# Routed experts of a two-layer block: gathered experts first, then all-token experts in row form with the small pairs between them

## The chip, the cores and the metric

The kernel runs on one core of one Trainium2 chip. The metric is the time of one execution on the device in microseconds (us).

## What is computed

Two blocks of two layers each run one after the other on 256 tokens of width 1024. The change touches only the experts of the second block, which both of its layers have:

```
N_EXPERTS = 16; TOP_K = 2; D_EXPERT = 512
def grouped_moe(x, router_w, router_bias, w_gate, w_up, w_down):
    xt = x.reshape(-1, d)
    ...
    combine = jnp.sum(one_hot(expert_idx, 16) * weights[..., None], axis=1)
    y = jnp.zeros(xt.shape)
    for e in range(N_EXPERTS):
        he = silu(xt @ w_gate[e]) * (xt @ w_up[e])
        y = y + combine[:, e:e + 1] * (he @ w_down[e])
    return y
```

Each token picks two experts of 16; `xt` is 256 x 1024, gate and up weights are 1024 x 512, down weights 512 x 1024. The result goes with the residual into a layer norm, and that into the next layer or out. All is float32. A product that needs more than one pass of TensorE's rounded type is made of three: a matrix is split into a high part (a rounded copy) and a low part (what is left), and high x high, high x low and low x high are added up.

## The kernel before

**Tiling.** Tokens lie in two tiles of 128. PSUM is eight banks of 128 x 512 (`PS`); banks 0 to 3 collect the experts' sum for the whole layer, banks 4 to 7 hold what is in work. Weights come from HBM in chunks of 128 x 1024 (512 KB) into `raw`, six places. ACT writes the chunk's high part (`whi`, `w3h`, `w4h`: five places), DVE subtracts and writes the low part (`wlo`, `w3l`, `w4l`).

**Experts by rank.** The router sorts the 16 experts by how many tokens they have. The first three (`ND`) can have any number and see all 256 tokens. The next five (`NL`) have at most 128, 104, 88, 76 and 64 places (`CAPS`); their tokens are gathered by matmuls with a 0/1 matrix (`pick`) into `xgh` and `xgl`, and their outputs scattered back by its transpose (`pickT`). The last eight have at most 64 tokens each and go in four pairs (`NP`): two experts side by side on the halves of the array, in plain float32, so that their weights are not split. A pair chunk is two DMAs of 512 KB into one slot of a ring (`ring`, three slots, `NSLOT`) and eight recorded matmul passes.

**The order.** Each engine runs the order in which its part is written, with semaphores between the engines; nothing is reordered by a scheduler. `gather` makes 32 units, four for each eighth of the width: two for the gathered experts, two for the pairs. Before it twelve small matmuls spread the all-token experts' routing weights over rows (`wrow`). `experts` then has two parts. First twelve steps of the all-token experts, each one 128-wide piece of the hidden width: weights stationary, the 256 tokens moving (`gate_up_half`, L2104), then the down projection (`down`, L2124). Four pair chunks lie between them in each step, in runs of one and two. After three steps a pair is done. Then come the gathered experts, five of them, in a software pipeline (`up_or_gate`, `down_e`, `turn_e`, `scatter`): for expert i up (4 chunks), scatter of i-2, gate (4), down of i-1 (4), then the transposes of i's hidden rows.

**ACT and DVE in the gathered part.** For each expert both engines have fixed duties between the splits of chunks: the silu of the gate (`silu_e`, L880) and the scaling by up and routing weight on DVE (`gated_e`, L1930), both after the last gate chunk; the copy and the subtraction of the transposed hidden rows (`hidden_e`, L884 and L1936); the copy and subtraction of the output (`out_e`). `split_e` (L867, L1923) splits the next chunk in the order of use. How many `split_e` stand ahead of each duty is written in the loop from L921 on. The DMA queue (SP) loads a chunk as soon as the split six chunks earlier is done (`large_load`).

Of the kernel before, what the change touches and what calls it, by code (L numbers as in the profile page):

```python
# [62 lines left out]
TURNS_E = 2  # L63
# [13 lines left out]
STEPS_D = 2 * TURNS_E * ND  # L77
PAIR_CHUNKS = 12
PC = PAIR_CHUNKS * NP
NSLOT = 3  # L80
UNIT_BANKS = (0, 1, 2, 3, 5, 6)
TURN_BANKS = (0, 1, 2, 3, 5)
NC = 12 * NL
PICKED = (NL, NL + 2, NB)
NRAW, NW = 6, 5
# [70 lines left out]
def both_blocks(nc, A, out):  # L156
    ctx = ExitStack()
    with ctx:
# [3 lines left out]
        def sem(name):  # L162
# [17 lines left out]
        wlo = sb("wlo", [P, 3, 1024], F32R)  # L180
        gs = sb("gs", [P, 2, S])
        h32 = sb("h32", [P, 2, S])
        hTh = sb("hTh", [P, 2, S], F32R)
# [22 lines left out]
        at = nc.alloc_sbuf_tensor_at  # L206
        memh = at("memh", [P, KB, S], F32R, offset=proj_at)
# [9 lines left out]
        wrow = at("wrow", [P, ND, S], F32, offset=pairs_at[0] + 4 * KB * 2 * P)  # L217
        ring = [at(f"ring{n}", [P, 1024], F32, offset=o) for n, o in enumerate((
            pairs_at[1] + 4 * KB * 2 * P, RA_at + 4 * (2048 + NB * S), tl_at, tl_at + 4 * 1024, xn_at, xn_at + 4 * 1024))]
        poh = at("poh", [P, 1024], F32R, offset=gain_at)  # L220
        pol = at("pol", [P, 1024], F32R, offset=gain_at + 4 * 1024)
        uw = sb("uw", [P, S])
# [4 lines left out]
        outh = xTh[:].rearrange("p k s -> p (k s)")[:, 0:D]  # L227
        outl = xTl[:].rearrange("p k s -> p (k s)")[:, 0:D]
        out2h = xTh[:].rearrange("p k s -> p (k s)")[:, D:2 * D]
        out2l = xTl[:].rearrange("p k s -> p (k s)")[:, D:2 * D]  # L230
        out_of = lambda i: (out2h, out2l, UB) if i == NL - 1 else (outh, outl, 6)
# [137 lines left out]
        ln_in = sem("ln_in")  # L369
# [96 lines left out]
        wrow_ready = sem("wrow_ready")  # L466
# [11 lines left out]
        def down_end(i):  # L478

            return 12 * i + 20 if i < NL - 1 else NC  # L480

# [6 lines left out]

        def e_w(n):

            if n % NW < 3:
                return whi[:, n % NW], wlo[:, n % NW]
            return (w3h[:], w3l[:]) if n % NW == 3 else (w4h[:], w4l[:])
# [22 lines left out]
        def _(sp):  # L516
# [44 lines left out]
            with sp.Fori(0, DEPTH) as l:  # L561
# [27 lines left out]
                sp.dma_start(par[:, 0], A["ln_x_w"][l].partition_broadcast(P)).then_inc(ln_in, 16)  # L589
                sp.dma_start(par[:, 1], A["ln_x_b"][l].partition_broadcast(P)).then_inc(ln_in, 16)  # L590
# [30 lines left out]
            for l in range(DEPTH):  # L621
# [37 lines left out]
                t0 = 4 * TURNS_FFN + ND * TURNS_E * l  # L659
                t_end = t0 + ND * TURNS_E  # L660
# [10 lines left out]

                at_d = [None]
                at_p = [None, None]

                def dense_load(u, m):

                    if u % (2 * TURNS_E) == 0 and m == 0:
                        at_d[0] = chosen(u // (2 * TURNS_E))
                    cols = slice(u % (2 * TURNS_E) * P, (u % (2 * TURNS_E) + 1) * P)
                    if m < 2:  # L680
                        src = w[("e_gate", "e_up")[m]][at_d[0]].rearrange("o (k p) f -> p (o k) f", p=P)[:, :, cols]
                    else:
                        src = w["e_down"][at_d[0], cols, :].rearrange("o f n -> f (o n)")
                    step_load(m, t0 + u // 2, u % 2, src)

                def pair_load(c):

                    p, part, slot = c // PAIR_CHUNKS, c % PAIR_CHUNKS, c % NSLOT
# [3 lines left out]
                    if c >= NSLOT:  # L692
                        hold(sp, p_used, PC * l + c - NSLOT + 1)
                    elif c:
                        hold(sp, gat_psum, UNITS * (l + 1))
                    for e in range(2):
                        dst = ring[2 * slot + e][:]
# [4 lines left out]

                n = 0
                at_l = [None, None]

                def large_load():

                    nonlocal n
# [2173 lines left out]
```

## Time and profile before

| | |
|---|---|
| time, median of 3 runs | 2420.82 us (2416.68 to 2422.79) |
| profiled execution: time, span | 2423.87 us, 2421.7 us |
| TensorE matmul busy | 2294.5 us, 95% |
| VectorE (DVE), ScalarE (ACT) busy | 1418.9 us (59%), 982.4 us (41%) |
| HBM read | 451.56 MB, 187 GB/s over the span |
| TensorE's granted clock, mean | 0.985 of full |
| one layer's expert stage | 311 us, twice |

The page is read from its first part, which gives the engines' shares, to the timeline, which gives for one engine the instructions in order of time with the idle time before them and who ended it. In the timeline a float32 matmul stands as two records, so "x8" is one pair chunk of four matmuls. A record's length reaches past the start of the next one, since matmuls are pipelined: what a matmul costs is the distance of starts. "PEclk" is the clock that TensorE was granted, where 1.00 is 2.4 GHz and 0.50 is 1.2 GHz.

### The profile page before, as it was taken

The page shows a single profiled execution, that of the slowest core. Times are in us where ns is not written, and L with a number is a line of the kernel's source. Part 1 is how long each engine was busy: PE and PEld are TensorE (multiplying, and loading weights), DVE is VectorE, ACT ScalarE, POOL GpSimd, SP SyncE. Part 2 cuts the span into 40 slices and gives each one's busy share as a digit, 9 for nine tenths or more (in the row PEclk, how much of TensorE's full clock was granted, in tenths as well). Part 3 has the DMA queues.
Part 4 walks back from the last instruction along what each step waited for, and adds up shares of the span by engine and source line. Part 5 has one row for each costly group of instructions (what it writes and reads, how often), then busy time and mean ns, then how long its engine had stood idle before and what let it go on. Part 6 is the DMA issues. An engine that isn't in the chain of part 4 may idle for free.

```text
span 2421.7 us, 37290 instructions
## 1 busy us (share of the span) xinstructions
PE 2294.5 (95%) x13918; PEld 1878.9 (78%) x13918; DVE 1418.9 (59%) x1893; ACT 982.4 (41%) x1245; POOL 101.6 (4%) x82
## 2 busy tenths in 40 slices
PE   9999999999999999999999898999999889999997
PEld 7998888899899888889988576866666677666664
DVE  5666767666666567666664356633348565533377
ACT  5554522444555453244443234332237333322264
POOL 0000023000000003200000000000000000000000
PEclk9999999999999999999999999999999999999998
DMA  6667501566566761046656242489989441599985
GB/s 194 187 187 218 169 10 35 170 186 182 158 182 185 222 192 44 1 145 186 187 178 189 91 157 91 148 287 338 331 297 335 163 157 61 193 340 342 316 307 205
DMA packets 386961, 458.02 MB, mean 189 GB/s; under 512 B 18542, under 2 KB 273170, under 8 KB 386706
## 3 DMA queue, kind: packets, MB, share of 16 engines
q1 hardware_dynamic: 381824, 446.35, 57.5%
q10 hardware_dynamic: 5010, 9.98, 1.3%
q8 instruction: 79, 1.29, 0.2%
q14 instruction: 48, 0.39, 0.0%
HBM read 451.56 MB, written 1.05 MB: 187 GB/s over the span
## 4 chain that ended last, share of the span: by engine, by line
PE 49%; issue 37%; DVE 7%; DMA 2%; POOL 2%; ACT 2%; SPq 1%; ACTq 0%; DVEq 0%; POOLq 0%; PEldq 0%
PE PS L2306 4%; PE PS L2114 4%; PE PS L2116 3%; PE PS L2115 3%; PE PS L2310 2%; PE PS L2392 2%; PE PS L2133 2%; PE PS L2394 2%; PE PS L2393 2%; PE PS L2134 2%; PE PS L2135 2%; PE PS L2243 2%; PE PS L2245 1%; PE PS L2244 1%; PE PS L2686 1%
## 5 line engine op out<-in xcount | busy, mean ns | idle before, releaser
L1312 DVE TENSOR_TENSOR wlo<-raw,whi 128x1024 fp32r<-128x1024 f32 x336 | 410.2, 1224 | 446.6 <-ACT whi L828 443.6
L828 ACT ACTIVATE whi<-raw 128x1024 fp32r<-128x1024 f32 x336 | 354.2, 1057 | 501.0 <-PE PS L2116 379.0
L2114 PE MATMUL PS<-xTh,whi 128*128 128x256 f32 x1792 | 512.8, 286 | 5.6 <-DVE xTl L1279 4.0
L2115 PE MATMUL PS<-xTl,whi 128*128 128x256 f32 x1792 | 506.8, 283 | 0.0
L2116 PE MATMUL PS<-xTh,wlo 128*128 128x256 f32 x1792 | 506.7, 283 | 0.0
L2114 PEld LDWEIGHTS PS<-xTh,whi 128*128 128x128 f32 x1792 | 343.0, 191 | 41.8 <-issue 32.7
L2115 PEld LDWEIGHTS PS<-xTl,whi 128*128 128x128 f32 x1792 | 343.2, 192 | 3.2
L2116 PEld LDWEIGHTS PS<-xTh,wlo 128*128 128x128 f32 x1792 | 343.2, 191 | 0.0
L2392 PE MATMUL PS<-whi,xTh 128*128 128x416 f32 (+2 forms) x480 | 181.9, 379 | 18.5 <-DVE xTl L1279 7.5
L2133 PE MATMUL PS<-whi,hTh 128*128 128x512 f32 x448 | 179.0, 400 | 4.3 <-DVE wlo L1312 4.3
L2394 PE MATMUL PS<-whi,xTl 128*128 128x416 f32 (+2 forms) x480 | 177.3, 369 | 0.0
L2393 PE MATMUL PS<-wlo,xTh 128*128 128x416 f32 (+2 forms) x480 | 176.5, 368 | 0.0
L2134 PE MATMUL PS<-wlo,hTh 128*128 128x512 f32 x448 | 175.9, 393 | 0.0
L2135 PE MATMUL PS<-whi,hTl 128*128 128x512 f32 x448 | 174.4, 389 | 0.0
L1305 DVE TENSOR_TENSOR wlo<-raw,whi 128x1024 fp32r<-128x1024 f32 (+2 forms) x92 | 107.3, 1177 | 108.7 <-ACT whi L841 107.3
L841 ACT ACTIVATE whi<-raw 128x1024 fp32r<-128x1024 f32 (+2 forms) x92 | 91.2, 1019 | 149.9 <-PE PS L2394 101.2
L2306 PE MATMUL PS<-ring,xgp 128*64 128x512 f32 x512 | 120.7, 602 | 4.1 <-DMA ring<-in_l_e_up_dram 3.6
L2392 PEld LDWEIGHTS PS<-whi,xTh 128*128 128x128 f32 x480 | 91.2, 190 | 38.6 <-issue 9.9
L2133 PEld LDWEIGHTS PS<-whi,hTh 128*128 128x128 f32 x448 | 84.4, 188 | 39.4 <-issue 17.8
L1376 DVE TENSOR_TENSOR wlo<-raw,whi 128x832 fp32r<-128x832 f32 (+1 forms) x80 | 83.6, 1063 | 53.5 <-ACT whi L979 50.9
L979 ACT ACTIVATE whi<-raw 128x832 fp32r<-128x832 f32 (+1 forms) x80 | 73.5, 930 | 100.9 <-PE PS L2394 51.6
L852 ACT ACTIVATE gs<-RB 128x256 f32<-128x256 f32 x88 | 37.0, 420 | 157.2 <-DVE RB L1321 157.2
(516 smaller groups left out, 3875.2 us busy)
## 6 DMA issues: line engine op xcount, KB each, us to landing
raw<-in_ffn_w_gate_dram SPq DMA_DIRECT2D x88, 512.0 KB, 5.3
raw<-in_ffn_w_up_dram SPq DMA_DIRECT2D x88, 512.0 KB, 6.3
raw<-in_ffn_w_down_dram SPq DMA_DIRECT2D x88, 512.0 KB, 3.7
raw<-in_l_e_gate_dram SPq DMA_DIRECT2D x64, 512.0 KB, 6.0
raw<-in_l_e_up_dram SPq DMA_DIRECT2D x64, 512.0 KB, 6.4
raw<-in_l_e_down_dram SPq DMA_DIRECT2D x64, 512.0 KB, 5.6
ring<-in_l_e_up_dram SPq DMA_DIRECT2D x64, 512.0 KB, 6.5
ring<-in_l_e_gate_dram SPq DMA_DIRECT2D x64, 512.0 KB, 6.7
```

The lines of the kernel that those rows point to most:

```text
L828: nc.scalar.activation(whi[:, m if slot is None else slot], raw[:, m, j], ACT.Copy).then_inc(hi_done[m], 1)
L1312: nc.vector.tensor_tensor(wlo[:, w], raw[:, m, j], whi[:, w].bitcast(F32), ALU.subtract).then_inc(lo_done[m], 1)
L2114: mm(out_, whi[:, m, ks], xTh[:, k, :], start=(k == 0), stop=False)
L2115: mm(out_, whi[:, m, ks], xTl[:, k, :], start=False, stop=False)
L2116: last = mm(out_, wlo[:, m, ks], xTh[:, k, :], start=False, stop=(k == KB - 1))
L2133: mm(out_, hTh[:, j, ts], whi[:, slot, ns], start=opens, stop=False, skip_group_check=True)
L2134: mm(out_, hTh[:, j, ts], wlo[:, slot, ns], start=False, stop=False, skip_group_check=True)
L2135: last = mm(out_, hTl[:, j, ts], whi[:, slot, ns], start=False, stop=False, skip_group_check=True)
L2306: last = mm(PS[rows, 6 + c // 4, :], xgp[p // 2][:, kk_, c0:c0 + HALF], ring[2 * slot + e][:, cs], start=(kk_ == 0), stop=(kk_ == KB - 1), ...
L2392: mm(out_, of[0][:, k, ts], whi[:, at[c], ws], start=(k == 0), stop=False)
L2393: mm(out_, of[0][:, k, ts], wlo[:, at[c], ws], start=False, stop=False)
L2394: last = mm(out_, of[1][:, k, ts], whi[:, at[c], ws], start=False, stop=(k == KB - 1))
```

## The change

The experts' two parts change places, and the all-token experts take another form.

- **Gather.** The twelve spreading matmuls and the copies into `wrow` are gone. The 16 units of the gathered experts come first, then the 16 of the pairs. The first split of weights no longer stands before the copies of `pickT`; three splits lie between the units' copies (after units 14, 20, 26 on ACT, 15, 21, 27 on DVE).
- **One chunk order.** `part_of` numbers 96 chunks of `raw`: 60 of the gathered experts and 36 of the all-token experts (12 each: 4 gate, 4 up, 4 down), dense chunk 0 between the last two down projections. Up to chunk 55 the five places for split chunks are used, then three (`w_slot`), since the other two become ring slots.
- **Row form.** `dense_part` holds the tokens stationary and moves 512 columns of weights: gate into banks 4 and 5, silu to `hd`, then up into the same banks; both are multiplied with the routing weight as a per-row scalar (`gated_d`), eight transposes (`dense_turn`), then down.
- **Pairs.** Five ring slots instead of three. The table `CPS` says how many of the 48 pair chunks follow each of the dense chunks 1 to 35, before and after a `dense_turn`; there are 22 runs, of which ten have three chunks. Slots 1 to 4 open as the tiles that they lie on fall free at the end of the gathered part.

```diff
-NSLOT = 3
+NSLOT = 5
+CPS = ((0, 0), (3, 0), (0, 0), (3, 0), (2, 0), (0, 0), (2, 0), (1, 1), (0, 0), (3, 0), (0, 0), (3, 0),
...
-NC = 12 * NL
+NC = PARTS * (NL + ND)
+N_DENSE = PARTS * NL - 4
...
+        def w_slot(n):
+            return n % 5 if n < N_DENSE else (n - N_DENSE + 1) % 3
```

ACT in the expert stage; DVE's code has the same sequence:

```diff
-                pair_out(NP - 1)
-                for i in range(NL + 1):
-                    if i < NL:
-                        if i:
-                            split_e()
-                            split_e()
-                            if i == 1:
-                                silu_e(0)
-                            hidden_e(i - 1)
...
-                        for _ in range(4 if i else 6):
-                            split_e()
-                        if i:
-                            split_e()
-                            split_e()
-                            silu_e(i)
-                            split_e()
-                            split_e()
...
+                for u in range(0, UNITS, 2):
+                    act.wait_ge(gat_psum, UNITS * l + u + 1)
+                    dst = xgh[:, u // 2] if u < 2 * KB else xgp[0][:, u // 2 - KB]
+                    nc.scalar.activation(dst, PS[:, UNIT_BANKS[u % 6], 0:dst.shape[1]], ACT.Copy).then_inc(gat_hi, 1)
+                    if u in (14, 20, 26):
                         split_e()
+                split_e(3)
+                for i in range(1, NL):
+                    split_e(2)
+                    if i == 1:
+                        silu_e(0)
+                    hidden_e(i - 1)
+                    split_e(2)
+                    if i > 1:
                         out_e(i - 2)
+                    split_e(6)
+                    silu_e(i)
+                    split_e(2)
+                split_e(4)
+                hidden_e(NL - 1)
+                out_e(NL - 2)
+                split_e(5)
+                out_e(NL - 1)
+                split_e()
```

TensorE's all-token chunk and its order:

```diff
+                    if part < 8:
+                        for k in range(2):
+                            kk_, ws = 2 * (part % 4) + k, slice(k * 512, (k + 1) * 512)
+                            for t in range(NT):
+                                ts = slice(t * P, (t + 1) * P)
+                                mm(PS[:, 4 + t, :], xTh[:, kk_, ts], hi[:, ws], start=(kk_ == 0), stop=False)
+                                mm(PS[:, 4 + t, :], xTh[:, kk_, ts], lo[:, ws], start=False, stop=False)
+                                last = mm(PS[:, 4 + t, :], xTl[:, kk_, ts], hi[:, ws], start=False, stop=(kk_ == KB - 1))
...
-                for p in range(NP):
-                    for s in range(3):
-                        u = 3 * p + s
-                        gate_up_half(t0 + u // 2, u % 2, 0)
...
+                for i in range(NL):
+                    up_or_gate(i, UB)
...
+                    up_or_gate(i, GB)
                     assert n == gate_end(i)
                     if i:
                         down_e(i - 1)
+                    turn_e(i)
+                dense_part(0)
+                scatter(NL - 2)
+                down_e(NL - 1)
+                for q in range(1, NQ):
+                    dense_part(q)
+                    if q == 1:
+                        scatter(NL - 1)
+                    if q in TURN_Q:
+                        pair_turn(TURN_Q.index(q))
+                    if q in SCATTER_Q:
+                        pair_scatter(SCATTER_Q.index(q))
+                    c = FIRST_CP[q]
+                    for k in range(CPS[q][0]):
+                        pair_chunk(c + k)
+                    if q % PARTS == 7:
+                        dense_turn(q // PARTS)
+                    for k in range(CPS[q][1]):
+                        pair_chunk(c + CPS[q][0] + k)
```

Two places of the order show what stands in a row. ACT before, around the silu (`gs`, 104 rows) and the copy of the transposed hidden rows (`hTh`) of gathered expert 1; chunk n goes to `whi` for n mod 5 of 0, 1, 2, to `w3h` for 3, to `w4h` for 4:

```order
L877 ACTIVATE w3h<-raw 128x1024
L877 ACTIVATE w4h<-raw 128x1024
L877 ACTIVATE whi<-raw 128x1024 x3
L882 ACTIVATE gs<-PS 104x512
L877 ACTIVATE w3h<-raw 128x1024
L877 ACTIVATE w4h<-raw 128x1024
L877 ACTIVATE whi<-raw 128x1024 x2
L886 ACTIVATE hTh<-PS 128x416
L877 ACTIVATE whi<-raw 128x1024
L877 ACTIVATE w3h<-raw 128x1024
L891 ACTIVATE xTh<-PS 128x1024
```

Ahead of the silu chunk 17 is split, and chunks 18 to 21 lie between silu and copy. The same place of ACT after the change:

```order
L892 ACTIVATE whi<-raw 128x1024 x3
L892 ACTIVATE w3h<-raw 128x1024
L892 ACTIVATE w4h<-raw 128x1024
L892 ACTIVATE whi<-raw 128x1024
L897 ACTIVATE gs<-PS 104x512
L892 ACTIVATE whi<-raw 128x1024 x2
L892 ACTIVATE w3h<-raw 128x1024
L892 ACTIVATE w4h<-raw 128x1024
L901 ACTIVATE hTh<-PS 128x416
L892 ACTIVATE whi<-raw 128x1024 x2
L905 ACTIVATE outh<-PS 128x1024
```

Ahead of the silu chunk 15 is split, the last of expert 1's gate, and chunks 16 to 19 lie between silu and copy. TensorE before, a single pair chunk (ring tiles against `xgp`) between the two kinds of all-token matmul:

```order
L2115 MATMUL PS<-xTl,whi 128x256
L2116 MATMUL PS<-xTh,wlo 128x256
L2306 MATMUL PS<-ring_66,xgp_60 64x512
L2306 MATMUL PS<-ring_67,xgp_60 64x512
L2306 MATMUL PS<-ring_66,xgp_60 64x512
L2306 MATMUL PS<-ring_67,xgp_60 64x512
L2133 MATMUL PS<-whi,hTh 128x512
L2134 MATMUL PS<-wlo,hTh 128x512
```

One chunk is four matmuls, and the down step follows. TensorE after the change, the first run of three chunks, behind dense chunk 1 and the scatter of the last gathered expert:

```order
L2340 MATMUL PS<-ring_0_63,xgp_61 64x512
L2340 MATMUL PS<-ring_1_64,xgp_61 64x512
L2340 MATMUL PS<-ring_0_63,xgp_61 64x512
L2340 MATMUL PS<-ring_1_64,xgp_61 64x512
L2340 MATMUL PS<-ring_0_65,xgp_61 64x512
L2340 MATMUL PS<-ring_1_66,xgp_61 64x512
L2340 MATMUL PS<-ring_0_65,xgp_61 64x512
L2340 MATMUL PS<-ring_1_66,xgp_61 64x512
L2340 MATMUL PS<-ring_0_67,xgp_61 64x512
L2340 MATMUL PS<-ring_1_68,xgp_61 64x512
L2340 MATMUL PS<-ring_0_67,xgp_61 64x512
L2340 MATMUL PS<-ring_1_68,xgp_61 64x512
```

Three slots of the ring are used up in one run, then dense chunk 2 follows.

## Rows read from the trace of the kernel before

**Rows 1.** Timeline of PE, both expert stretches (start us, us, ..., [idle before]).
```profile
1585.44 0.35 PE L2114 MATMUL PS<-xTh,whi 128*128 128x256 f32 x1 [0.67 <-ACT xgp L1245]
...
1896.15 0.39 PE L2288 MATMUL PS<-xTl,pickT 64*128 64x512 f32 x1
...
2097.64 0.35 PE L2114 MATMUL PS<-xTh,whi 128*128 128x256 f32 x1 [0.67 <-ACT xgp L1245]
...
2408.23 0.39 PE L2288 MATMUL PS<-xTl,pickT 64*128 64x512 f32 x1
```

**Rows 2.** Timeline of PE, a pair chunk, a down step, two pair chunks.
```profile
1762.99 1.94 PE L2306 MATMUL PS<-ring,xgp 128*64 128x512 f32 x8
1764.85 0.50 PE L2133 MATMUL PS<-whi,hTh 128*128 128x512 f32 x1
...
1767.80 3.65 PE L2306 MATMUL PS<-ring,xgp 128*64 128x512 f32 x16
```

**Rows 3.** Timeline of PE, matmuls of a gathered expert, twelve starts apart.
```profile
1802.31 0.40 PE L2243 MATMUL PS<-whi,xgh 128*128 128x512 f32 x1
...
1805.11 0.40 PE L2243 MATMUL PS<-whi,xgh 128*128 128x512 f32 x1
```

**Rows 4.** Timeline of PE, two waits for DVE in layer 0.
```profile
1796.19 0.50 PE L2243 MATMUL PS<-whi,xgh 128*128 128x512 f32 x1 [2.47 <-DVE wlo L1927]
...
1886.29 0.45 PE L2265 MATMUL PS<-whi,hTh 128*64 128x512 f32 x1 [1.51 <-DVE hTl L1939]
```

**Rows 5.** Timelines of PE, ACT, DVE behind the first gathered expert's transposes.
```profile
1808.13 0.66 PE L2277 MATMUL PS<-tab,h 128*128 128x128 f32 x4 [1.47 <-DVE h L1933]
1808.54 0.48 PE L2243 MATMUL PS<-w3h,xgh 128*104 128x512 f32 x1
...
1811.68 0.48 PE L2243 MATMUL PS<-whi,xgh 128*104 128x512 f32 x1
...
1808.82 0.60 ACT L886 ACTIVATE hTh<-PS 128x512 fp32r<-128x512 f32 x1 [1.53 <-PE PS L2277]
...
1810.40 2.36 DVE L1927 TENSOR_TENSOR wlo<-raw,whi 128x1024 fp32r<-128x1024 f32 x2 [0.26 <-ACT whi L877]
```

**Rows 6.** Timelines of PE and ACT behind the second gathered expert's gate.
```profile
1820.10 0.40 PE L2265 MATMUL PS<-whi,hTh 128*128 128x512 f32 x1
...
1823.16 0.50 PE L2265 MATMUL PS<-w3h,hTh 128*128 128x512 f32 x1
...
1820.30 0.60 ACT L882 ACTIVATE gs<-PS 104x512 f32<-104x512 f32 x1 [1.26 <-PE PS L2245]
```

**Rows 7.** Timeline of PE, head of the gather in layer 0.
```profile
1562.99 1.50 PE L2189 MATMUL PS<-tab,par 128*128 128x128 f32 x12
...
1568.73 0.73 PE L2217 MATMUL PS<-pick,xrh 128*128 128x460 f32 x2 [1.57 <-ACT pickT L1238]
```

**Rows 8.** Groups of instructions by line and shape (xcount | busy us, mean ns).
```profile
L1970 DVE SCALAR_TENSOR_TENSOR par<-par,PS 128x512 f32<-128x512 f32 x4 | 3.0, 749 | 7.4 <-ACT par L906 7.4
```

**Rows 9.** Busy time by window (us, engines, PEclk, DMA share, GB/s).
```profile
1600.00:1620.00 20.00, 20.00 (x120) 13.01 (x117) 5.95 (x8) 4.04 (x5) 0.00 (x0) 1.00 1.06 369
```

**Rows 10.** Timeline of PE, two waits elsewhere in the kernel.
```profile
834.77 0.46 PE L2392 MATMUL PS<-whi,xTh 128*128 128x416 f32 x1 [3.19 <-DVE xTl L1279]
...
1308.14 1.10 PE L2686 MATMUL PS<-tl,raw 128*128 128x256 f32 x4 [2.78 <-DMA raw<-in_l_xkv_dram]
```

**Rows 11.** Busy time by window, behind those two waits.
```profile
835.00:836.00 1.00, 1.00 (x5) 0.96 (x5) 1.00 (x4) 1.00 (x4) 0.00 (x0) 0.65 0.99 349
836.00:837.00 1.00, 1.00 (x5) 0.95 (x4) 1.00 (x4) 0.58 (x1) 0.00 (x0) 0.50 0.86 305
837.00:838.00 1.00, 1.00 (x5) 0.95 (x4) 1.00 (x2) 0.00 (x0) 0.00 (x0) 0.50 0.20 75
838.00:839.00 1.00, 1.00 (x5) 0.96 (x4) 0.00 (x0) 0.10 (x1) 0.00 (x0) 0.64 0.00 0
1309.00:1310.00 1.00, 1.00 (x7) 0.87 (x6) 0.71 (x4) 0.16 (x1) 0.00 (x0) 1.00 1.06 412
```

More of the change, by code:

```diff
@@ L751, in _ @@
-                while n < NC:
-                    large_load()
+                while n < NRAW:
+                    part_load()
+                pair_load(0)
+                while n < N_DENSE + 4:
+                    part_load()
+                pair_load(1)
+                pair_load(2)
+                part_load()
+                part_load()
+                pair_load(3)
+                pair_load(4)
+                while n < N_DENSE + 12:
+                    part_load()
+                for step in range(1, NQ):
+                    if n < NC:
+                        part_load()
+                    for c in range(FIRST_CP[step], FIRST_CP[step] + sum(CPS[step])):
+                        if c + NSLOT < PC:
+                            pair_load(c + NSLOT)
@@ new lines, in experts @@
+                split_e(4)
+                hidden_e(NL - 1)
+                out_e(NL - 2)
+                split_e(5)
+                out_e(NL - 1)
+                split_e()
+                for q in range(1, NQ):
+                    if q % PARTS == 7:
+                        gated_d(q // PARTS)
+                    if n < NC:
+                        split_e()
+                    c = FIRST_CP[q]
+                    for k in range(CPS[q][0]):
+                        pair_step(c + k)
+                    if q % PARTS == 7:
+                        hidden_d(q // PARTS)
+                    for k in range(CPS[q][1]):
+                        pair_step(c + CPS[q][0] + k)
@@ L2205, in gather @@
                 for u in range(UNITS):
[L2206 to L2208 removed]
+                    k, bank = u // 2 % KB, UNIT_BANKS[u % 6]
+                    ks = slice(k * P, (k + 1) * P)
                     if u < 6:
@@ L2305, in pair_chunk @@
                                 kk_, c0 = 2 * (c % 4) + k, P * (p % 2) + HALF * e
-                                last = mm(PS[rows, 6 + c // 4, :], xgp[p // 2][:, kk_, c0:c0 + HALF], ring[2 * slot + e][:, cs], start=(kk_ == 0), stop=(kk_ == KB - 1),
+                                last = mm(PS[rows, 6 + c // 4, :], xgp[p // 2][:, kk_, c0:c0 + HALF], ring[slot][e][:, cs], start=(kk_ == 0), stop=(kk_ == KB - 1),
                                           skip_group_check=True)
@@ L2349, in experts @@
[L2349 to L2354 removed]
+                for i in range(NL):
+                    up_or_gate(i, UB)
+                    if i == 0:
+                        pe.wait_ge(gat_hi, UNITS // 2 * (l + 1))
+                        pe.wait_ge(gat_lo, UNITS // 2 * (l + 1))
+                    else:
```

541 lines of the change are left out of this document (238 added, 303 removed).

## Prediction, made before the changed kernel was run

> **What bounds the kernel now.** I read the page first: TensorE is busy for 95% of the span, DVE for 59%, ACT for 41%. Then the timeline of TensorE over the expert stage of each of the two layers, since the change touches that alone. Each stretch lasts 310.9 us from its first matmul to its last (1585.44 to 1896.15, 2097.64 to 2408.23, and 0.2 to the end of the issue slot) [rows 1]. Inside, TensorE goes from matmul to matmul with few holes. DMA moves up to 369 GB/s in a window where TensorE never waits [rows 9], so the transfers keep up but have little to spare. So the bound is TensorE's own order, and the question for the change is twofold: how much TensorE work the new order has, and where TensorE now waits for the split of a weight chunk (ACT writes the high part, DVE subtracts to get the low part).
>
> **Prices on TensorE.** Twelve matmuls of 512 columns start over 2.80 us (1802.31 to 1805.11), 0.233 each, in longer stretches 0.2325; a large chunk of six takes 1.39, a dense chunk of twelve 2.79 [rows 3]. A pair chunk takes 1.86 from its start to the next group's (1762.99 to 1764.85); the record of two chunks is 3.65 against 1.94, so a further chunk adds 1.71. The down step behind it takes 2.95 instead of 2.79 [rows 2]. So each run of pair chunks costs 0.15 + 0.15 beside 1.71 a chunk.
>
> **The gathered experts, in the new place but first without new waits.** Expert 0: 48 matmuls, 11.2, then its transposes with the wait of 1.47 and 0.41 to the next start [rows 5]: 13.1. From 1808.54 [rows 5] the three rounds and the fourth, up to the start of the down projection of expert 4 at 1886.29 [rows 4], take 77.7 in the layer before, and stay. Then dense chunk 0 (2.8), a scatter of eight (1.9) and the last down projection (5.6). Sum 101.1.
>
> **The mixed stage.** 35 dense chunks at 2.79: 97.7. 48 pair chunks at 1.71: 82.1. By the table CPS they lie in 22 runs, 22 x 0.30 = 6.6 (before: 32 runs). Four scatters of pairs and one of a gathered expert, 8 x 0.2325 each: 9.3. Four groups of four transposes at 0.4 [rows 5] and three of eight at 0.8: 4.0. Sum 199.7. Added wait: the all-token hidden rows now need two scalings of 0.75 [rows 8] before their transposes; for experts 0 and 1 a pair chunk of 1.86 covers them, for expert 2 only four transposes do, so 1.5 + 0.2 - 0.4 = 1.3. The copies behind the transposes (two of ACT at 0.60 [rows 5], two of DVE) lie beside one or two pair chunks and add nothing; without that cover they would add some 1.5 each. Together 201.0.
>
> So without new waits a layer's experts would take 302.1, 8.8 less than 310.9. What goes are stalls of the layer before, such as 2.47 before the third large chunk [rows 4], and ten switches between the kinds; the wait of 1.51 before the last down projection [rows 4] stays and is in the 77.7.
>
> **The lead that is lost.** This is the step that decides. ACT and DVE work strictly in the order written. Before, ACT has split 18 large chunks when it comes to the silu of expert 1, and 22 when it comes to the copy of that round's transposes; TensorE has then used 16 and 20. It runs on over two chunks (2.8) while ACT and DVE do silu, scaling and the next split. The order view of the changed kernel shows ACT with 16 and 20 at these places: the first loop now does 6 splits before expert 1 instead of 8 and nothing restores the two. The first chunk that TensorE wants stands behind the silu (or the copy) on ACT, and behind the scaling (or the subtraction) on DVE. The rows of before hold the price, since there the third chunk takes that very way. Behind the transposes of expert 0 the wanted start is 1808.54; ACT's copy starts at 1808.82, DVE's first split behind it runs from 1810.40, and the third chunk starts at 1811.68: 3.14 later [rows 5]. Behind the gate of expert 1 the wanted start is 1820.10, silu starts at 1820.30, the third chunk at 1823.16: 3.06 later [rows 6]. After the change the first chunk starts there. Four gates (experts 1 to 4) and four transposes (0 to 3; narrower copies, so a little less, 3.0) give 8 x 3.04 = 24.3 a layer. Two smaller things cancel: the third chunk no longer waits its 3.04 - 2.79 = 0.25 eight times (-2.0), but where ACT and DVE also move an expert's output (three times) DVE has three pieces of 1.13 apart before the third chunk against 2.79 of TensorE (+1.8). Nothing else has to wait on TensorE's behalf in that time: DMA gains from it.
>
> A layer's experts: 302.1 + 24.3 - 0.2 = 326.2, against 310.9: +15.3, twice +30.6.
>
> **The gather.** Removed: the twelve small matmuls that spread the routing weights (1.50 busy, 1.34 from start to start), the wait of 1.57 for ACT's copies, which stood behind two weight splits [rows 7], and 0.67 before the first matmul, which waited for the last gathered tile [rows 1]; it now writes another bank. Layer 0: -3.6. In layer 1 TensorE did not wait for ACT's copies: -2.0. Now ACT and DVE make three splits inside the gather; six banks lie between a unit and its reuse, so I take nothing. At the end the first token tile is signalled six matmuls before the end instead of four: -0.5 a layer. Together -6.6.
>
> **DMA.** The mixed stage takes 50.3 MB of pairs and 18.3 MB of dense weights in 201 us, 341 GB/s, of which five pair chunks and three dense ones (6.8 MB) can be there at its start. The ring of five pair slots gives every load at least 12.8 us from the release of its slot to its use by the prices above; three pair chunks at 369 GB/s [rows 9] take 8.5. The layer before had the lead of three slots. I take no wait; the bound is that each of the ten runs of three waits half a microsecond, 5 a layer.
>
> **TensorE's clock.** Sixteen new waits of about 2.9 as the profile counts them (start to start 3.3 less the record of 0.39). Elsewhere a wait of 3.19 is followed by a granted clock of 0.65, 0.50, 0.50, 0.64, which is 1.2 GHz for about 3.4 us and costs 1.7; a wait of 2.78 is followed by 1.00, 2.4 GHz [rows 10, 11]. The new waits lie between, nearer the lower. I take two or three falls in sixteen: +4. Ends: none (0), all sixteen (+27). The Trainium skill (TensorE: Matmul & The Clock Gate, HAM oscillation) describes a matmul stream that falls to the half clock at every tile since a wait stands between its bursts. By that page the term would be near +27, by the rows it is near 0 to +4.
>
> **Sum.** +30.6 - 6.6 + 4 = +28. The profiled execution has a span of 2421.7 and a time of 2423.87, 3 above the median of 2420.82; so 2449.7 for the span and 2449 for the median.
>
> **Rivals.**
> The clock falls often. If eight or more of the sixteen waits end in the slow level, it costs 14 to 27 instead of 4: 2459 to 2472. For it speaks that 2.9 is close to 3.19; against it that 2.78 left the clock alone. The page of the Trainium skill named above would give its upper end; the trace lies between the two.
> DMA cannot feed the runs of three. Ten waits of 0.5 a layer: +10, 2459. For it: 341 wanted against 369 at best. Against it: five slots where the layer before ran with three, and no load that is asked for later than 12.8 before its use.
> The lead does not bind (the other side). If TensorE still finds the first chunk split, neither the 48.6 of both layers' waits nor the 4 of the clock are paid, and the time is 2420.8 - 17.6 - 6.6 = 2397. It decides by one thing: whether ACT stands two chunks ahead at a silu. The order view says it does not. If only one of the two places bound (the gates, say), 24.3 and half the clock's 4 would go, about 2423: no change.
>
> **Chances.** Forecast as described (2440 to 2456) 0.72; clock falls often 0.10; DMA or another unseen wait 0.11; one place only 0.03; lead does not bind 0.04. The range that holds 8 in 10 takes in the clock's and DMA's lower cases: 2438 to 2462. A measurement here tells 0.3%, 7 us, from no change. Slower 0.93, same 0.03, faster 0.04.
>
> **What the changed profile would show.** Right: four rows of TensorE per layer with about 2.9 idle before a down projection (releaser DVE's split) and four before an up projection; experts' stretch near 326; no such waits later. TensorE's busy share falls from 95% to about 93%. The granted clock in the gathered stage tells rival one; idle before pair chunks with a DMA as releaser tells rival two. Wrong: large chunks that start at once behind a gate.

## The result, and the profile after

The changed kernel is slower: 1.0242 of the time before, 95% interval 1.0208 to 1.0276. Its median over four executions is 2479.12 us against 2418.75 for the kernel before; one of the four, 3293.09, was disturbed: the ratio leaves it out, and the median of the other three is 2474.56. The profiled execution took 2483.68, its span is 2481.9; before, the span was 2421.7. So 60.2 us are to be found in the two traces. The forecast was +28.

First the page of the changed kernel: its span, the busy time of the engines, and the rows of PE, PEclk and GB/s over 40 equal slices.

```profile
span 2481.9 us, 36018 instructions
...
PE 2315.3 (93%) x13338; PEld 1868.3 (75%) x13366; DVE 1396.7 (56%) x1821; ACT 984.1 (40%) x1241; POOL 101.6 (4%) x82
...
PE   9999999999999999999999899888999898888997
...
PEclk9999999999999999999999899988999999988999
...
GB/s 190 190 188 226 146 1 59 173 191 185 156 183 190 221 153 7 43 186 178 187 173 160 98 136 115 212 228 266 380 339 253 144 128 99 195 227 307 365 345 158
```

TensorE is busy for 93% of the span instead of 95%, as forecast. The new dips lie in the slices in which the gathered experts stand (from 1577 and from 2124; a slice is 62 us). Transfers now come in a hill: up to 380 GB/s averaged over a slice, in the mixed stage; before, they ran at 322 and 315 GB/s over the whole of the experts' stretches.

Next the busy time by window, one window for each stage of the changed kernel (window, its length, PE busy with the number of matmuls, granted clock, DMA share, GB/s): the kernel up to the gather, the gather, the gathered experts of layer 0, the mixed stage of layer 0, what lies between the layers, then gathered experts and mixed stage of layer 1, and the end.

```profile
0.00:1557.45 1557.45, 1485.15 (x9566) 0.99 0.51 149
1557.45:1576.56 19.11, 19.11 (x167) 1.00 0.75 257
1576.56:1705.11 128.55, 102.96 (x382) 0.85 0.67 228
...
1715.37:1924.07 208.70, 204.26 (x885) 0.98 0.86 315
1924.07:2123.59 199.52, 178.01 (x990) 0.98 0.36 120
2123.59:2249.28 125.69, 100.10 (x383) 0.88 0.68 229
...
2259.53:2469.27 209.74, 205.25 (x885) 0.98 0.83 306
2469.27:2481.90 12.63, 0.00 (x0) 0.63 0.21 83
```

With the 10.3 of dense chunk 0, the scatter and the last down projection (left out between the stages), the experts take 347.5 and 345.7, against 310.7 and 310.6 before [rows 1]: 71.9 of loss, of which the rest of the kernel gives 11.7 back. Three things stand in the two rows of the gathered experts. PE is busy for 103 of 128.55 us; the granted clock is 0.85 and 0.88; and the time of the two layers differs by 2.9 though they do the same work, which goes with the difference of their clocks. The same stretch before ran at 1.00.

The waits of TensorE in the gathered experts of layer 0 (waited for, total us, times, longest), and behind "..." those of the rest of the layer's experts:

```profile
PE PS L2254 <- DVE wlo L1930: 8.9, 3, 3.0
PE PS L2235 <- DVE wlo L1930: 5.6, 2, 2.8
PE PS L2254 <- DVE w3l L1930: 3.0, 1, 3.0
PE PS L2235 <- DVE w3l L1930: 2.9, 1, 2.9
PE PS L2235 <- DVE w4l L1930: 2.7, 1, 2.7
PE PS L2266 <- DVE h L1936: 1.5, 1, 1.5
...
PE PS L2276 <- DVE outl L1947: 3.3, 1, 3.3
PE PS L2323 <- DVE hd L1953: 1.1, 1, 1.1
```

The first five rows are the eight waits of the forecast: four before a down projection (L2254), four before an up projection (L2235), 2.72 to 2.98 each, for the low part of a split chunk. Layer 1 has the same eight. They answer to the single waits of [rows 4]. The row of L2276 was not forecast: the scatter of the last gathered expert waits 3.3 us.

What a wait leaves behind it, in the timeline of PE: the first rows after the wait of 2.89, and after the one before that scatter.

```profile
1592.91 0.75 PE L2235 MATMUL PS<-w3h,xgh 128*104 128x512 f32 x1 [2.89 <-DVE w3l L1930]
1593.46 0.63 PE L2236 MATMUL PS<-w3l,xgh 128*104 128x512 f32 x1
1593.88 0.63 PE L2237 MATMUL PS<-w3h,xgl 128*104 128x512 f32 x1
...
1599.17 0.39 PE L2235 MATMUL PS<-whi,xgh 128*104 128x512 f32 x1
...
1721.57 0.67 PE L2276 MATMUL PS<-outh,pickT 64*128 64x512 f32 x1 [3.31 <-DVE outl L1947]
```

From start to start a matmul takes 0.42 to 0.43 instead of 0.23, until 1598.6: TensorE runs at 1.2 GHz instead of 2.4, with a granted clock of 0.50 from 1592.0 to 1598.8.

### The profile page after: what moved, and what is told of

The parts are those of the page before. It is cut to its first block, busy times and chain, and to the rows that moved or that the text cites. A ratio compares the mean times of both kernels' runs of the same rounds, so it can differ in the third digit from the quotient of the medians.

```text
span 2481.9 us, 36018 instructions
## 1 busy us (share of the span) xinstructions
PE 2315.3 (93%) x13338; PEld 1868.3 (75%) x13366; DVE 1396.7 (56%) x1821; ACT 984.1 (40%) x1241; POOL 101.6 (4%) x82
## 4 chain that ended last, share of the span: by engine, by line
PE 51%; issue 37%; DVE 7%; ACT 2%; POOL 2%; DMA 1%; SPq 1%; ACTq 0%; DVEq 0%; POOLq 0%; PEldq 0%
PE PS L2340 5%; PE PS L2344 2%; PE PS L2297 2%; PE PS L2416 2%; PE PS L2235 2%; PE PS L2418 2%; PE PS L2237 2%; PE PS L2417 2%; PE PS L2236 2%; PE PS L2298 2%; PE PS L2119 2%; PE PS L2118 2%; PE PS L2117 2%; PE PS L2299 2%; PE PS L2710 1%
## 5 line engine op out<-in xcount | busy, mean ns | idle before, releaser
L1322 DVE TENSOR_TENSOR wlo<-raw,whi 128x1024 fp32r<-128x1024 f32 x264 | 322.2, 1223 | 225.5 <-ACT whi L846 222.4
L2117 PE MATMUL PS<-xTh,whi 128*128 128x256 f32 x1408 | 399.9, 284 | 4.5 <-DVE xTl L1289 4.3
L2119 PE MATMUL PS<-xTh,wlo 128*128 128x256 f32 x1408 | 399.1, 283 | 0.0
L2118 PE MATMUL PS<-xTl,whi 128*128 128x256 f32 x1408 | 399.1, 283 | 0.0
L846 ACT ACTIVATE whi<-raw 128x1024 fp32r<-128x1024 f32 x264 | 277.4, 1053 | 227.1 <-PE PS L2119 218.8
L1930 DVE TENSOR_TENSOR wlo<-raw,whi 128x1024 fp32r<-128x1024 f32 x148 | 177.9, 1221 | 252.9 <-ACT whi L892 252.9
L2117 PEld LDWEIGHTS PS<-xTh,whi 128*128 128x128 f32 x1408 | 270.6, 192 | 9.0 <-DVE xTl L1289 5.3
L2118 PEld LDWEIGHTS PS<-xTl,whi 128*128 128x128 f32 x1408 | 270.6, 192 | 3.2
L2119 PEld LDWEIGHTS PS<-xTh,wlo 128*128 128x128 f32 x1408 | 270.6, 192 | 0.0
L892 ACT ACTIVATE whi<-raw 128x1024 fp32r<-128x1024 f32 x148 | 153.4, 1054 | 261.1 <-PE PS L2299 169.8
L2136 PE MATMUL PS<-whi,hTh 128*128 128x512 f32 x352 | 139.0, 395 | 4.4 <-DVE wlo L1322 4.4
L2137 PE MATMUL PS<-wlo,hTh 128*128 128x512 f32 x352 | 138.0, 392 | 0.0
```

The lines of the kernel that those rows point to most:

```text
L846: nc.scalar.activation(whi[:, m if slot is None else slot], raw[:, m, j], ACT.Copy).then_inc(hi_done[m], 1)
L892: nc.scalar.activation(e_w(n)[0], e_raw(n), ACT.Copy).then_inc(e_hi, 1)
L1322: nc.vector.tensor_tensor(wlo[:, w], raw[:, m, j], whi[:, w].bitcast(F32), ALU.subtract).then_inc(lo_done[m], 1)
L1930: TTop(e_w(n)[1], e_raw(n), e_w(n)[0].bitcast(F32), ALU.subtract).then_inc(e_lo, 1)
L2117: mm(out_, whi[:, m, ks], xTh[:, k, :], start=(k == 0), stop=False)
L2118: mm(out_, whi[:, m, ks], xTl[:, k, :], start=False, stop=False)
```

## The experiments

The theory: the lost lead of two split chunks makes the eight waits a layer, and the waits bring the clock down. The rivals: the new order or its transfers cost the time and the waits are a symptom; or the clock falls for a reason of its own. A third question is the unforeseen scatter wait. ACT's and DVE's programs have the same order of splits, so each edit of it is shown once and stands in both.

### The lead given back

```diff
-split_e(3)
+split_e(5)
 for i in range(1, NL):
     ...
-split_e(4)
+split_e(2)
 hidden_e(NL - 1)
```

> The changed kernel with its two split chunks given back: on ACT and on VectorE five large chunks are split between the gather and the loop over the gathered experts instead of three, and two instead of four behind that loop. TensorE's program is untouched. Theory (lost lead, and a clock that falls behind the waits): the sixteen waits of about 3.0 us from start to start go (48.6), and with them the stretches at the lower clock that stand behind fifteen of them in the trace (13 to 16 us a layer in the profiled execution); the third chunk of a group waits 0.25 again (+4). From 2477 that gives 2400 to 2412, granted clock back at 0.983 or more. Rival (the waits alone; the clock falls for another reason of the new order): 2428 to 2433 with the clock still near 0.972. Rival (transfers): the lead only moves the wait to the landing of the raw chunks, above 2440, with DMA named before ACT's splits. The wait of 3.3 before the scatter of the last gathered expert stays in all of them.

Measured: 2407.65, ratio 0.9947 (0.9924 to 0.9971) to the kernel before, granted clock 0.984. The gathered experts take 90.46 and 90.47 instead of 128.55 and 125.69; between the transposes of expert 0 and those of expert 4 no wait longer than 0.2 us is left. The theory's range holds it; both rivals are out. The same TensorE program is some 70 us faster with two chunks of lead, and faster than the kernel before.

### The scatter of the last gathered expert, alone

```diff
-split_e(5)
+split_e(4)
 out_e(NL - 1)
-split_e()
+split_e(2)
```

> The changed kernel with one thing moved: behind the loop over the gathered experts ACT and VectorE split four chunks, then move the output of the last gathered expert, then split two, instead of five, the output, one. It is the price of the one wait that the forecast did not name: TensorE stands 3.31 and 3.36 us before the scatter of that output (releaser VectorE's outl), and the next 8 scatter matmuls and the pair chunks behind them run at 0.64 to 0.67 of the clock. Theory (the output stands behind a split whose raw chunk lands late, since four pair loads are ahead of it): the wait and its clock go, 3.3 + 3.3 to 4.3 a layer, so 2477 - 14 = 2463 (2460 to 2466). Rival (the output is late by itself, two moves of 1.1 to 1.3 and the semaphores between them): the wait only shrinks, and 2474 to 2478 stays.

Measured: 2468.39 (2464.76 to 2472.81), a little above what was expected, ratio 1.0208 (1.0180 to 1.0236). The intervals of this ratio and of the changed kernel's overlap, so the times alone do not settle it. The trace does: the mixed stage is 202.14 and 202.15 instead of 208.70 and 209.74, at clock 1.00 instead of 0.98. The windows of the mixed stage of both layers:

```profile
1708.93:1911.07 202.14, 201.01 (x886) 1.00 0.88 325
...
2248.20:2450.35 202.15, 201.01 (x885) 1.00 0.85 315
```

So the place costs 6.6 and 7.6, 14.2 in all, about half of it the wait.

### Both edits

> Both edits together: two split chunks of lead for the gathered experts, and the output of the last gathered expert one split earlier. TensorE's program is that of the changed kernel. If the two places are independent and hold all that the change lost, the time is that of the sum without new waits, 2 x 302.1 for the experts (before: 2 x 310.9) and some 7 to 12 less in the gather and at the ends: 2388 to 2396, about 1% under the kernel before. Rival (the new order costs more than its count of matmuls, through transfers or the runs of three pair chunks): above 2405, with idle time of TensorE before pair chunks or dense chunks in the mixed stage.

Measured: 2392.57, ratio 0.9893 (0.9864 to 0.9923). Busy time by window of this kernel, gathered experts and mixed stage of both layers:

```profile
1573.06:1663.57 90.51, 87.34 (x383) 1.00 0.91 321
...
1673.80:1875.94 202.14, 201.01 (x886) 1.00 0.88 327
...
2075.27:2165.77 90.50, 87.31 (x383) 1.00 0.91 321
...
2176.00:2378.15 202.15, 201.02 (x885) 1.00 0.86 317
```

A layer's experts take 302.9, which is the cost of the new order by itself. The forecast's count was 302.1. The rival (the new order costs more than its matmuls) is out: TensorE is busy for 201.0 of 202.1 us of the mixed stage.

### The waits filled

```diff
 pe.wait_ge(eo_lo, NB * l + i)
+if i < NL - 1:
+    warm(11, 6)
...
 turn_e(i)
+if i < NL - 1:
+    warm(11, UB)
...
 if q == 1:
+    for _ in range(11):
+        mm(PS[:, 0, :], zero[:, 0:P], zero[:], start=False, stop=False, skip_group_check=True)
     scatter(NL - 1)
```

Here `warm(n, bank)` issues n matmuls on zeros into a bank that is free at that place.

> The changed kernel with its waits as they are, but TensorE has work in them: eleven matmuls on zeros (bf16, 512 columns, about 0.24 us each, 2.6 us together) before the down projections of gathered experts 0 to 3, before the up projections of experts 1 to 4, and before the scatter of the last one; they add nothing to the result. They fit into the waits of 2.7 to 3.3, so the real matmuls start at the same moment as before. It separates the two parts of a wait: the standing itself, and the stretch at the lower clock behind it. Theory (half of what the change lost is the clock, 27 to 36 us in all): 2441 to 2452, granted clock back at 0.983 or more while ACT and VectorE keep their times. Rival (the lower clock behind the waits costs little, since the splits would have held TensorE anyway): 2470 to 2477 with a clock near 0.985. Rival (the clock falls whatever stands in the waits): 2477, clock 0.972.

Measured: 2452.90, ratio 1.0149 (1.0119 to 1.0180), granted clock 0.990. First the timeline of PE at the first filled wait, then the windows of the gathered experts of both layers.

```profile
1580.43 2.54 PE L2080 MATMUL PS<-zero 128*128 128x512 bf16 x11
1583.49 0.48 PE L2235 MATMUL PS<-w3h,xgh 128*104 128x512 f32 x1 [0.52 <-DVE w3l L1930]
1583.81 0.39 PE L2236 MATMUL PS<-w3l,xgh 128*104 128x512 f32 x1
...
1567.14:1681.64 114.50, 107.14 (x471) 1.00 0.71 247
...
2100.39:2214.84 114.45, 107.12 (x470) 1.00 0.72 247
```

The real matmul still starts 3.06 after the first zero one, and the next one is at full speed. The gathered experts take 114.5 in both layers. So the whole parts into three: 90.5 of work, 24.0 of waiting (114.5 - 90.5), and 14.0 and 11.2 of lower clock (128.55 - 114.50, 125.69 - 114.45). The clock's theory holds, though the median is 1 above its range. The fill did nothing for the scatter: there the zeros took 2.55 of a wait that grew to 5.0 (a wait of 2.48 is left behind them), and the mixed stage still took 208.8. TensorE had come sooner and the scatter could not: what it waits for comes at a time of its own.

### Why the scatter waits

```diff
 pair_load(1)
 pair_load(2)
 part_load()
 part_load()
+part_load()
+part_load()
 pair_load(3)
 pair_load(4)
```

> The kernel with its lead given back, and one more edit on the loading queue alone: two raw chunks (the second and third of the first dense expert's gate) are asked for before the fourth and fifth pair chunks instead of behind them. ACT's and VectorE's programs stay, so the output of the last gathered expert still stands behind the split of the third dense chunk. Theory (that split waits 4.16 for its raw chunk, which landed 10 us after it was asked for, behind the pair loads, so the wait before the scatter is a transfer's): the wait of 3.7 and the clock behind it go, 7.0 a layer in the trace, 2407.7 - 14 = 2394. Rival (the order on ACT and VectorE is the cause, whenever the chunk lands): 2407. Rival (DMA moves 388 GB/s there and is full, so that the delay only moves to a pair chunk): 2400 to 2407 with idle time before a pair chunk.

Measured: 2391.79, ratio 0.9891 (0.9874 to 0.9907); the mixed stage is 202.1. ACT's timeline, in the kernel with the lead alone (first two rows) and in this one (last two): a split, and the high part of the last output behind it.

```profile
1679.29 1.06 ACT L892 ACTIVATE whi<-raw 128x1024 fp32r<-128x1024 f32 x1 [4.51 <-DMA raw<-in_l_e_gate_dram]
1680.25 1.00 ACT L905 ACTIVATE outh<-PS 64x1024 fp32r<-64x1024 f32 x1
```

```profile
1671.43 1.06 ACT L894 ACTIVATE whi<-raw 128x1024 fp32r<-128x1024 f32 x1 [0.32 <-PE PS L2258]
1672.75 1.02 ACT L907 ACTIVATE outh<-PS 64x1024 fp32r<-64x1024 f32 x1 [0.26 <-PE PS L2258]
```

The split in front of the output waited 4.51 for a raw chunk. With that chunk asked for before two of the pair loads, it is there and the output follows at once. So the wait belonged to the loading order: a transfer behind four pair loads, a split that waits for it, an output behind the split, the scatter behind the output. Two links were cut, each alone: the first here, and the third where the output was moved one split earlier. The rival that the full DMA would move the delay to a pair chunk is out: no pair chunk waits.

### The lead taken from the kernel before

```diff
-for _ in range(4 if i else 6):
+for _ in range(4):
     split_e()
 ...
-    for _ in range(3):
+    for _ in range(5):
         split_e()
     hidden_e(i - 1)
```

> The kernel before, with the edit that the change made to the lead and nothing else: four large chunks are split ahead of expert 1 instead of six, two more ahead of the last hidden rows. Order on TensorE, buffers and transfers are those of before. Theory (the lead by itself costs what the change lost in the gathered experts): a layer gets the eight waits (24.0 by the run with filled waits, 114.5 less 90.5) and the clock behind them (11 to 14): 35 to 38 a layer, so 2419 + 73 = 2489 to 2495, with a granted clock near 0.97. Rival (the waits belong to the new place or buffers of the gathered experts, not to the lead): 2419 to 2425.

Measured: 2487.78, ratio 1.0294 (1.0274 to 1.0314), +70. The waits of TensorE in its gathered experts of layer 0:

```profile
PE PS L2265 <- DVE wlo L1927: 8.9, 3, 3.0
PE PS L2243 <- DVE wlo L1927: 5.6, 2, 2.8
PE PS L2265 <- DVE w3l L1927: 3.0, 1, 3.0
PE PS L2243 <- DVE w3l L1927: 2.9, 1, 2.9
PE PS L2243 <- DVE w4l L1927: 2.7, 1, 2.7
```

Row for row these are the waits of the changed kernel. The rival (they belong to the new place or its buffers) is out. The time is 1 us under the range that was expected.

### A lead of one chunk

The two edits, with `split_e(4)` and `split_e(3)` around the loop in place of 5 and 2.

> Lead of one chunk instead of none or two: both earlier edits together, but with four chunks split ahead of the loop and three behind it. The chunk that TensorE wants after a gate or the transposes is then split, the next one is not. Theory (a wait is 3.04 less what TensorE can still do, 1.39 for one chunk): 1.65 before the second chunk instead of 3.04 before the first, eight times a layer, 13.2; and such a short wait, below the 2.78 that left the clock alone in the kernel before, costs no clock. From 2392.6: 2419 (2415 to 2422), clock near 0.988. Rival (any hole in this stream costs the clock its 1.5 again): 2440 to 2446, clock near 0.975. Rival (the splits catch up by themselves, as one chunk is enough): 2393 to 2396.

Measured: 2417.07, ratio 0.9996 (0.9982 to 1.0010). Three rows of TensorE's waits in the gathered experts of layer 0, and the windows of that stretch in both layers:

```profile
PE PS L2235 <- DVE wlo L1930: 3.6, 4, 1.4
PE PS L2254 <- DVE wlo L1930: 3.0, 2, 1.5
PE PS L2235 <- DVE w3l L1930: 1.8, 2, 1.4
...
1570.93:1674.35 103.42, 87.95 (x383) 1.00 0.80 275
2089.35:2192.79 103.44, 88.01 (x382) 1.00 0.80 277
```

The waits are 1.33 to 1.53 and cost 12.9 a layer (103.4 - 90.5; expected 13.2). The clock stays at 1.00 through all sixteen. So in both layers together the first missing chunk costs 26 us of waiting (24.5 in the medians), the second another 22 of waiting and 25 of clock.

### How often, and how long, a wait must be to cost the clock

One wait a layer (the first kernel of this part: both edits, and the lead taken away at the gate of expert 2 only):

```diff
-split_e(6)
+split_e(4 if i == 2 else 6)
 silu_e(i)
-split_e(2)
+split_e(4 if i == 2 else 2)
```

> Both earlier edits together (two chunks of lead, output one split earlier), and then the lead taken away at one place a layer only, the gate of expert 2: two of the six splits ahead of its silu now stand behind it. One wait of about 3.0 a layer in a stretch where TensorE otherwise never stands. It asks if the clock falls behind one such wait, or only where they come every 14 us. Theory (each wait of 2.9 as the profile counts it is enough): a first record above 0.6 us behind it, granted clock 0.5 to 0.75 in the window after it, 4.5 a layer, about 2401. Rival (a single wait leaves the clock alone, as the one of 2.78 did in the kernel before, and the falls of the changed kernel come from their frequency): 1.00 behind it, 3.0 a layer, about 2398.

Measured: 2397.01 in one execution. The timeline of PE at the wait, in layer 0 and in layer 1, two rows each:

```profile
1618.94 0.45 PE L2254 MATMUL PS<-w3h,hTh 128*104 128x512 f32 x1 [2.98 <-DVE w3l L1930]
1619.23 0.39 PE L2255 MATMUL PS<-w3l,hTh 128*104 128x512 f32 x1
...
2123.01 0.73 PE L2254 MATMUL PS<-w3h,hTh 128*104 128x512 f32 x1 [2.98 <-DVE w3l L1930]
2123.54 0.63 PE L2255 MATMUL PS<-w3l,hTh 128*104 128x512 f32 x1
```

The same wait at the same place of the program: once the clock stays, once it falls. Neither theory nor rival is right. The length of a wait does not decide alone. Other single waits in the traces say the same. The first row below is from the changed kernel, early in the program, and the clock stays at 1.00 behind it. The second is from the kernel with four ring slots (below), at the very place of the wait of 2.78 in [rows 10], and the clock behind it is 0.50 until 1316.6:

```profile
211.34 0.46 PE L2416 MATMUL PS<-whi,xTh 128*128 128x416 f32 x1 [3.05 <-DVE xTl L1289]
...
1310.66 0.76 PE L2709 MATMUL PS<-tl,raw 128*128 128x256 f32 x1 [2.92 <-DMA raw<-in_l_xkv_dram]
```

Then shorter waits, sixteen of them again: the changed kernel with the output moved, and `warm(3, ...)` or `warm(1, ...)` in place of eleven, none before the scatter.

> The changed kernel with the output of the last gathered expert one split earlier (2468 by its own run) and its lead still missing, and three matmuls on zeros (0.24 us each, 0.7 together) in each of the sixteen waits instead of eleven. TensorE starts its real work at the same moment; it stands 2.0 to 2.3 instead of 2.7 to 3.0. It asks how long a hole of this stream costs the clock. Known so far: with 0.35 to 0.5 and with 1.4 to 1.5 nothing was lost, with 2.72 to 2.98 the clock was lost 48 times in 50. Theory (a hole must be near three microseconds long): no loss, the 25 to 28 us of the clock come back, 2441 (2438 to 2446). Rival (a hole of two is enough): 2464 to 2470, granted clock near 0.974.

> As the run with three, but one matmul on zeros (0.24 us) in each wait: TensorE stands 2.4 to 2.7. Theory of a sharp length: either all of the falls stay (2465) or all go (2441). Rival (it depends on where the hole lies, as the two layers of the run with one hole showed for one and the same wait of 2.98): some of the sixteen fall, in between.

Measured: 2464.67 (ratio 1.0196, 1.0167 to 1.0224) with three, and 2461.91 in one execution with one. The windows of the gathered experts, with three zeros:

```profile
1576.98:1699.89 122.91, 102.62 (x401) 0.90 0.69 234
2112.30:2235.72 123.42, 103.13 (x401) 0.90 0.70 233
```

The idle times are 2.07 to 2.24 there (2.50 to 2.89 with one zero matmul), and 8.4 and 9.0 above the 114.5 of the filled waits remain, at clock 0.90. The theory (a wait must be near three microseconds) fell; the time lies in the rival's range. In the trace the clock is below full in 13 of 16 such intervals with three zeros, and in 13 of 16 with one. So with one zero, too, neither all falls stayed nor all went; its rival (some of them) holds.

### The slack of the transfers

Both edits, with `NSLOT = 4` and without the fifth early pair load.

> Both earlier edits together (2392.6), with four slots for pair chunks instead of five. It measures the slack of the transfers in the mixed stage, where DMA moves 331 to 391 GB/s and TensorE waits for no pair chunk. By the counts a load then has 3 pair chunks and 2 dense ones (10.9 us) at the tightest between the release of its slot and its use, and three pair chunks at 369 GB/s take 8.5. Theory (the ring has a slot to spare): no change, 2390 to 2396. Rival (DMA is the next bound, and the five slots are what hides it): TensorE waits before pair chunks with DMA as the releaser, 5 us a layer or more, 2402 and above.

Measured: 2396.43 (2386.72 to 2400.61), ratio 0.9896 (0.9861 to 0.9931). The mixed stage of layer 0:

```profile
1681.69:1883.85 202.16, 201.03 (x885) 114.47 (x886) 59.64 (x57) 51.39 (x59) 0.00 (x0) 1.00 0.89 327
```

202.16 with four slots, 202.14 with five. The ring has a slot to spare. The median is 0.4 above the range of the theory and the executions spread by 14 us; the profiled one lost 29.0 us to the lower clock ahead of the gather, against 18.8 in that of the kernel with five slots.

## Why the forecast was wrong, step by step

The direction and the deciding mechanism were right, the size was not: +28 against some +60. In the profiled executions, us for both layers:

| step | forecast | measured | from |
|---|---|---|---|
| work of the new order, without the new waits | -17.6 | -15.5 | 302.9 a layer against 310.65 |
| waits of the lost lead | +48.2 | +47.9 | 114.5 - 90.5 |
| the clock behind them | +4 | +25.3 | 14.05 + 11.24 |
| scatter of the last gathered expert | 0 | +14.2 | 6.6 + 7.6 |
| gather, between the layers, end, and what lies ahead of the gather | -6.6 | -11.7 | windows before and after |
| sum | +28 | +60.2 | |

**What bounds the kernel, and the prices.** Right. TensorE's own order is the bound, and counted matmuls at the prices of [rows 2] and [rows 3] gave 302.1 for a layer that takes 302.9. The mixed stage takes 1.1 more than counted, and the gathered part gives 0.4 back. Runs of three pair chunks take 5.30, of two 3.58, of one 1.87, as 0.15 + 1.71 a chunk says.

**The lost lead.** Right, in place, number and size: eight a layer, 24.1 forecast, 24.0 measured, from the 3.14 and 3.06 of [rows 5] and [rows 6]. The restored lead, the half lead and the old order without its lead each give the cost that this working gives.

**The clock.** This term failed: two or three falls in sixteen were taken, 4 us; it was 25. The bounds (0 to 27) held it, and so did the rival "the clock falls often", which had a chance of 0.10. The step that failed is the reading of [rows 10, 11]: a wait of 3.19 with a fall and one of 2.78 without were read as two sides of a length. They were two single waits, far from others. Behind waits of 2.72 to 2.98 that come two to a round of some 28 us, the clock was below full in 47 of 48 intervals (the changed kernel, the one with the output moved, the old order without lead); behind one such wait a layer in one case of two; behind waits of 2.07 to 2.24 in 13 of 16; behind waits of 1.33 to 1.53 in none of 16. That the wait of 2.78 kept the clock was no sign of its length: 2.92 at the same place in another kernel's trace did not, and 3.05 elsewhere did. The Trainium skill (TensorE: Matmul & The Clock Gate, HAM oscillation) describes a stream of bursts with a wait between them and the clock down at each; its waits, for transfers, are longer (3 to 5 us). The waits of 2.72 to 2.98 here behave like it, at 25 of the 27 that were worked out as its end; those of 1.33 to 1.53 do not. The clock events of the traces add up to 18.8 and 15.4 us of lost clock in the two stretches, but the cost was 14.0 and 11.2. Of the difference, 1.5 and 1.3 lie inside the waits, where TensorE does nothing. Some more is that a slow first chunk gives ACT and DVE the time for the third, before which TensorE stands 0.4 us three times a layer in the kernel with filled waits; the rest stays open.

**The scatter.** The forecast had its eight matmuls and no wait. It looked for the limit of the transfers in the runs of three pair chunks and gave each load there 12.8 us; that was right, and a run with one slot fewer changed nothing. But it did not follow the raw chunks past the new place of the pair loads in the loading queue. One of them lands 13.6 us after it is asked for in layer 0 and 11.3 in layer 1, and its split stands ahead of an output that TensorE wants. The wait is 3.3, and the clock behind it doubles the price. The forecast counted for the lead what stands behind a waiting instruction, and did not do it here.

**The gather and the rest.** Forecast -3.6, -2.0 and -0.5 twice. The gather of layer 0 went from 24.47 to 19.11, -5.4; before, it held one fall of the clock (0.93 granted, 1.7 us), after none, so the removed work is worth 3.7. Between the layers, with the gather of layer 1: 201.49 to 199.52, -2.0. Another 3.5 lie ahead of the gather, where both programs are the same (1560.97 and 1557.45); they are no effect of the change, but 3.4 of lost clock (25.6 and 22.2). The last 0.8 are at the end (13.47 and 12.63).

**The range.** 2438 to 2462 held the forecast's clock and DMA cases one at a time. Each unknown had its bound in the text (27 for the clock, 10 for transfers), but with the clock at 25 and a transfer's wait together the time is above both.

## What to carry to other kernels

When work is moved, count at every point where a strictly ordered engine turns from preparing to something else how many prepared pieces lie ahead, and compare it with before; one number, 18 or 16 splits ahead of a silu, was worth 70 us here, and was not part of what the change was about. Where a wait of TensorE of about three microseconds comes back every ten to twenty, count the lower clock behind each one: here it cost 1.6 us a wait, and still 1.1 where the waits were 2.1 to 2.2. Do not read a threshold from two single waits. A load that is put into a shared queue delays everything behind it, so follow the next raw chunk to its split and to what stands behind the split.

## What the runs showed of the hardware

- In the gathered experts, waits of 1.33 to 1.53 us left the granted clock at 1.00 sixteen times out of sixteen; waits of 2.07 to 2.24 did not in thirteen of sixteen. Nothing between was tried there. The same wait of 2.98 at the same instruction of two layers ended once at full and once at half clock.
- These are no thresholds for other places. The wait of 2.47 in [rows 4], once a layer in the kernel before, left the clock at 1.00 in both layers. The wait of 1.57 in [rows 7], which stands behind some 50 matmuls of one column, was followed by a fall at 1569.2.
- Eleven bf16 matmuls on zeros in each wait of 3.0 us brought the clock from 0.85 to 1.00 and gave back 14.0 us of 128.5, with every wait still there.
- The stretch ahead of the gather, with the same instructions, took 1560.97 us in the profiled execution of the kernel before, and 1548.13 in that of the kernel with filled waits. The clock lost was 25.6 and 13.7; less that, both are within 1 us of 1535. Over the profiled executions of all thirteen kernels the stretch took 1548.1 to 1561.9 and, less the clock lost, 1532.3 to 1535.8. So most of its spread is time at the lower clock.
- DMA ran at a share of 1.04 and 1.00 for 74 us (391 GB/s from 1676 to 1700, 372 from 1700 to 1750, in the kernel with both edits) while TensorE waited for none of it.
